# Two-layer encoder trunk on one core: the rings of split weight tiles made four deep and filled by whole tiles, and three unsplit tiles at the head of the second layer's projection

## What is computed

```python
q = einsum(h, w_q); sc = einsum(q, sub_keys)            # 8 heads, 2 sides, 128 keys each
v1, i1 = top_k(sc side 0, 16); v2, i2 = top_k(sc side 1, 16)
top_v, top_pos = top_k(all sums v1 + v2, 16)            # 16 experts of 16384 per head
gates = softmax(top_v)
a = gelu(einsum(u_tab[expert], h)) * gates
out = einsum(a, v_tab[expert])
```

## Time and profile before

| | us |
|---|---|
| median of three runs | 2061.69 |
| lowest, highest | 2059.86, 2061.74 |
| the profiled execution, its own time | 2065.37 |
| its span, first to last instruction | 2063.4 |
| PE, VectorE, ScalarE busy | 2018.4, 1487.8, 1054.8 |
| second expert product, first layer | 360.20 |
| second expert product, second layer | 348.40 |

### The profile page before, as it was taken

How to read it: one execution, slowest core, us unless ns; L and a number is a source line. 1 busy time by engine, 2 the same in 40 slices (tenths; PEclk the granted TensorE clock), 3 DMA queues, 4 the chain that set the end, 5 groups by cost and what they waited for, 6 DMA issues and landing times.

```text
span 2063.4 us, 43464 instructions
## 1 busy us (share of the span) xinstructions
PE 2018.4 (98%) x12678; PEld 1805.7 (88%) x12678; DVE 1487.8 (72%) x3743; ACT 1054.8 (51%) x2059; POOL 27.7 (1%) x56
## 2 busy tenths in 40 slices
PE   7989999999999999999999999999999999999997
PEld 6748899999999877777779689999999998888886
DVE  5662778877777688888875348786777767777776
ACT  2032245755555555555544424566555555555554
POOL 0000000000000000000000000000000000000000
PEclk9999999999999999999989999999999999999998
DMA  9861288865655899999820333777565577777774
GB/s 377 343 236 46 87 279 288 251 189 177 175 171 175 277 325 327 322 328 323 279 102 31 154 117 121 229 219 212 172 176 175 171 207 245 242 240 241 241 242 150
DMA packets 170904, 446.79 MB, mean 217 GB/s; under 512 B 19024, under 2 KB 85840, under 8 KB 166880
## 3 DMA queue, kind: packets, MB, share of 16 engines
q1 hardware_dynamic: 163472, 392.65, 59.6%
q0 software_dynamic: 7376, 53.45, 6.6%
HBM read 409.32 MB, written 36.70 MB: 216 GB/s over the span
## 4 chain that ended last, share of the span: by engine, by line
PE 94%; ACT 2%; DVE 2%; DMA 1%; issue 1%; DVEq 0%; ACTq 0%; SPq 0%
PE bank L492 93%; ACT big L931 1%; DMA big<-in_w_mod 1%; PE bank L631 1%; DVE raw L1097 0%; DVE big L1192 0%; PE bank L811 0%; DMA cst<-in_consts 0%; DVE big L1114 0%; DVE wmod_ring L1114 0%; DVE x_lo L1106 0%; DVE big L1527 0%; ACT L991 0%; ACT big L949 0%; ACT raw L878 0%
## 5 line engine op out<-in xcount | busy, mean ns | idle before, releaser
L1356 DVE TENSOR_TENSOR lo<-raw,hi 128x512 fp32r<-128x512 f32 x1024 | 702.5, 690 | 346.4 <-ACT hi L985 342.1
L985 ACT ACTIVATE hi<-raw 128x512 fp32r<-128x512 f32 x1024 | 642.8, 630 | 444.1 <-PE bank L492 430.2
L492 PE MATMUL bank<-x_hi,hi 128*128 128x256 f32 x2152 | 622.2, 289 | 3.9 <-ACT x_hi L876 1.8
L492 PE MATMUL bank<-x_hi,lo 128*128 128x256 f32 x2152 | 610.1, 283 | 0.0
L492 PE MATMUL bank<-x_lo,hi 128*128 128x256 f32 x2152 | 606.1, 283 | 0.0
L492 PEld LDWEIGHTS bank<-x_hi,hi 128*128 128x128 f32 x2152 | 413.6, 192 | 6.8 <-issue 4.2
L492 PEld LDWEIGHTS bank<-x_hi,lo 128*128 128x128 f32 x2152 | 413.6, 192 | 0.0
L492 PEld LDWEIGHTS bank<-x_lo,hi 128*128 128x128 f32 x2152 | 411.7, 192 | 0.0
L492 PE MATMUL bank<-hi,a_hi 128*128 128x512 f32 x1024 | 401.3, 392 | 3.4 <-issue 1.7
L492 PE MATMUL bank<-hi,a_lo 128*128 128x512 f32 x1024 | 398.8, 389 | 0.0
L492 PE MATMUL bank<-lo,a_hi 128*128 128x512 f32 x1024 | 398.4, 389 | 0.0
(11 more groups left out here) (159 smaller groups left out, 1344.4 us busy)
## 6 DMA issues: line engine op xcount, KB each, us to landing
raw<-in_u SPq DMA_DIRECT2D x256, 512.0 KB, 3.9
raw<-in_v SPq DMA_DIRECT2D x256, 512.0 KB, 4.6
s_store<-work SPq DMA_DIRECT2D x256, 128.0 KB, 3.7
wmod_ring<-s_store SPq DMA_DIRECT2D x256, 128.0 KB, 3.7
wmod_ring<-in_w_mod SPq DMA_DIRECT2D x54, 512.0 KB, 5.7
big<-in_w_mod SPq DMA_DIRECT2D x40, 512.0 KB, 6.3
big<-in_w_q POOLq DMA_DIRECT2D x16, 1024.0 KB, 7.1
big<-in_w_in POOLq DMA_DIRECT2D x6, 2048.0 KB, 14.4
```

The lines of the kernel that those rows point to most:

```text
L492: return nc.tensor.matmul(o, w, x, start=start, stop=stop, skip_group_check=free)
L985: f(hi[:, r % 2, c], raw[:, r, c], ACT.Copy).then_inc(s[l]["hi_done"], 1)
L1356: v.tensor_tensor(lo[:, r % 2, c], raw[:, r, c], hi[:, r % 2, c].bitcast(F32), ALU.subtract).then_inc(s[l]["lo_done"], 1)
```

## The change

`hi` and `lo` become rings of four tiles (`SPLITS`), filled and released by whole tiles; step `n` of ScalarE splits tile `n + 3`. All counts of `hi_done`, `lo_done` and `w_used` are in tiles, and the loops of PE turn over four tiles. In the second expert product the order of VectorE's step stays `weigh`, `lower`, `lower_a`, and `weigh` and `lower_a` stay two steps ahead; `a_hi`, `a_lo` stay rings of two. In the second projection the first three tiles are plain float32 products of the normalised input (which is now written as such), and `x_hi`, `x_lo` are made while they run. The first input weights of the first layer come as 1 MB after four modulation tiles, 1 MB after 15, and the rest from 16 on. The memory for the deeper rings comes from the space that GpSimd's DMA descriptors use (2048 bytes instead of the default).

```diff
-SPLITS = 2
+SPLITS = 4
...
+PLAIN_TILES = 3
...
-                    sp.wait_ge(s[l]["lo_done"], 2 * n - 6)
+                    sp.wait_ge(s[l]["lo_done"], n - 3)
                     load_u(n, n % 4)
...
                 def down_loads(j, i, r, fetches=True):
-                    sp.wait_ge(s[l]["lo_done"], STREAM - 6 + 2 * j)
+                    sp.wait_ge(s[l]["lo_done"], NKEY - 3 + j)
                     load_v(j, r)
                     if fetches:
                         fetch(j + 1, (r + 1) % 4, i + (1 if r == 3 else 0))
...
-                        if n < 3:
-                            pool.wait_ge(s[0]["mod_tile"], (4, EARLY - 2, EARLY)[n])
+                        if n == 0:
+                            pool.wait_ge(s[0]["mod_tile"], 4)
+                            pool.dma_start(big[:, 0:2 * D], w[:, 0:2 * D]).then_inc(win_in[6], 16)
+                            pool.wait_ge(s[0]["mod_tile"], EARLY - 1)
+                            b = 2 * D
+                        if n == 1:
+                            pool.wait_ge(s[0]["mod_tile"], EARLY)
                         pool.dma_start(big[:, b:e], w[:, b:e]).then_inc(win_in[n], 16)
                     pool.dma_start(big[:, BIAS_AT[0]:BIAS_AT[0] + nb], a["bias0"]).then_inc(bias_in, 16)
...
+                for m in range(PLAIN_TILES):
+                    weights_in(m)
+                    for k in range(KT):
+                        if m == 0:
+                            pe.wait_ge(norms["h_ready"], KT * 2 + k + 1)
+                        last = mm(bank[m][:, 0:T], w_qk(1, m, k), hT[:, k, :], k == 0, k == KT - 1)
+                    last.then_inc(s[1]["wt_used"], 1)
+                pe.wait_ge(s[1]["ph_done"], KT)
+                pe.wait_ge(s[1]["pl_done"], KT)
+                for m in range(PLAIN_TILES, QK_TILES[1]):
...
-                    o = bank[4 + r][:, 0:T]
-                    for h in range(2):
-                        pe.wait_ge(s[l]["hi_done"], 2 * n + h + 1)
-                        pe.wait_ge(s[l]["lo_done"], 2 * n + h + 1)
-                        for k in range(h * KT // 2, (h + 1) * KT // 2):
-                            c = slice(k * P, (k + 1) * P)
-                            mm(o, hi[:, r, c], x_hi[:, k, :], k == 0, False)
-                            mm(o, hi[:, r, c], x_lo[:, k, :], False, False)
-                            last = mm(o, lo[:, r, c], x_hi[:, k, :], False, k == KT - 1)
-                        last.then_inc(s[l]["w_used"], 1)
+                    o = bank[4 + r % 2][:, 0:T]
+                    pe.wait_ge(s[l]["hi_done"], n + 1)
+                    pe.wait_ge(s[l]["lo_done"], n + 1)
+                    for k in range(KT):
+                        c = slice(k * P, (k + 1) * P)
+                        mm(o, hi[:, r, c], x_hi[:, k, :], k == 0, False)
+                        mm(o, hi[:, r, c], x_lo[:, k, :], False, False)
+                        last = mm(o, lo[:, r, c], x_hi[:, k, :], False, k == KT - 1)
+                    last.then_inc(s[l]["w_used"], 1)
...
                     pe.wait_ge(s[l]["ah_done"], j + 1)
                     pe.wait_ge(s[l]["al_done"], j + 1)
+                    pe.wait_ge(s[l]["hi_done"], NKEY + j + 1)
+                    pe.wait_ge(s[l]["lo_done"], NKEY + j + 1)
                     for h in range(2):
-                        pe.wait_ge(s[l]["hi_done"], STREAM + 2 * j + h + 1)
-                        pe.wait_ge(s[l]["lo_done"], STREAM + 2 * j + h + 1)
                         c = slice(h * HALF, (h + 1) * HALF)
                         for t in range(TT):
                             o, tok = bank[2 * t + h][:, :], slice(t * P, (t + 1) * P)
-                            mm(o, a_hi[:, r, tok], hi[:, r, c], first, False, True)
-                            mm(o, a_hi[:, r, tok], lo[:, r, c], False, False, True)
-                            last = mm(o, a_lo[:, r, tok], hi[:, r, c], False, end, True)
-                        last.then_inc(s[l]["w_used"], 1)
+                            mm(o, a_hi[:, r % 2, tok], hi[:, r, c], first, False, True)
+                            mm(o, a_hi[:, r % 2, tok], lo[:, r, c], False, False, True)
+                            last = mm(o, a_lo[:, r % 2, tok], hi[:, r, c], False, end, True)
+                    last.then_inc(s[l]["w_used"], 1)
 
                 pe.wait_ge(s[l]["xh_done"], l + 1)
                 pe.wait_ge(s[l]["xl_done"], l + 1)
...
-                if l == 1:
-                    for w in range(2):
-                        for h in range(2):
-                            split_in(w, h)
...
-                def split(n, r, h, round_, wait=True):
+                def split(n, r, round_, wait=True):
                     act.wait_ge(raw_in[r], 16 * (round_ + 1) + 16 * l * (STREAM // RAWS))
                     if wait:
-                        act.wait_ge(s[l]["w_used"], 2 * n + h - 3)
-                    c = slice(h * HALF, (h + 1) * HALF)
-                    f(hi[:, r % 2, c], raw[:, r, c], ACT.Copy).then_inc(s[l]["hi_done"], 1)
+                        act.wait_ge(s[l]["w_used"], n - 3)
+                    f(hi[:, r], raw[:, r], ACT.Copy).then_inc(s[l]["hi_done"], 1)
 
                 def gelu(n, r, round_, wait=True):
-                    act.wait_ge(s[l]["w_used"], 2 * n + 2)
+                    act.wait_ge(s[l]["w_used"], n + 1)
                     if wait:
                         act.wait_ge(s_out[r], 16 * round_ + 16 * l * (NKEY // STAGES))
                     f(work[:, r, :], bank[4 + r % 2][:, 0:T], ACT.Gelu).then_inc(s[l]["s_gelu"], 1)
 
                 def up_step(n, r, round_, wait=True):
-                    nr, nround = (r + 2) % 4, round_ + (r + 2) // 4
-                    split(n + 2, nr, 0, nround)
+                    split(n + 3, (r + 3) % 4, round_ + (r + 3) // 4, wait or r > 0)
                     gelu(n, r, round_, wait)
-                    split(n + 2, nr, 1, nround)
 
                 def up_steps(lo, hi):
...
                 copy_keys(PH - 1)
+                split(2, 2, 0, False)
...
-                def down_step(j, r, round_):
-                    nr, nround = (r + 2) % 4, round_ + (r + 2) // 4 + NKEY // 4
-                    for h in range(2):
-                        split(NKEY + 2 + j, nr, h, nround)
-                    split_a(j + 2, r, nr)
+                def down_step(j, a, r, round_):
+                    if j is not None:
+                        split(NKEY + 3 + j, (r + 3) % 4, round_ + (r + 3) // 4 + NKEY // 4)
+                    split_a(a, r, (r + 2) % 4)
 
                 with act.Fori(0, NKEY // 4 - 1) as i:
                     for r in range(4):
-                        down_step(4 * i + r, r, i)
+                        down_step(4 * i + r, 4 * i + r + 2, r, i)
                 for r in range(2):
...
-                    if i == 2 and k:
-                        lower_x(k - 1)
-                if i == 2:
-                    lower_x(KT - 1)
-
-            def lower_x(k):
-                dve.wait_ge(norms["h_ready"], KT * 2 + k + 1)
-                v.scalar_tensor_tensor(out=x_lo[:, k, :], in0=hT[:, k, :], scalar=mod[1][:, k:k + 1], in1=x_hi[:, k, :].bitcast(F32),
-                                       op0=ALU.add, op1=ALU.subtract).then_inc(s[1]["pl_done"], 1)
...
             def project_split():
+                for k in range(KT):
+                    dve.wait_ge(s[1]["ph_done"], k + 1)
+                    v.tensor_tensor(x_lo[:, k, :], hT[:, k, :], x_hi[:, k, :].bitcast(F32), ALU.subtract).then_inc(s[1]["pl_done"], 1)
                 for w in range(WIN_TILES):
-                    if w + 2 < WIN_TILES:
-                        lower_in(w + 2, 0)
...
-                def lower(n, r, h):
-                    dve.wait_ge(s[l]["hi_done"], 2 * n + h + 1)
-                    c = slice(h * HALF, (h + 1) * HALF)
-                    v.tensor_tensor(lo[:, r % 2, c], raw[:, r, c], hi[:, r % 2, c].bitcast(F32), ALU.subtract).then_inc(s[l]["lo_done"], 1)
+                def lower(n, r):
+                    dve.wait_ge(s[l]["hi_done"], n + 1)
+                    v.tensor_tensor(lo[:, r], raw[:, r], hi[:, r].bitcast(F32), ALU.subtract).then_inc(s[l]["lo_done"], 1)
...
-                    for half in range(2):
-                        lower(NKEY + n, n, half)
+                    lower(NKEY + n, n)
                     lower_a(n, n, n)
-
-                def down_step(j, r, round_, mods=None):
+                lower(NKEY + 2, 2)
+
+                def down_step(j, r, round_, mods=None, left=True):
                     weigh(j + 2, (r + 2) % 4, round_ + (r + 2) // 4)
-                    for half in range(2):
-                        lower(NKEY + 2 + j, (r + 2) % 4, half)
+                    if left:
+                        lower(NKEY + 3 + j, (r + 3) % 4)
                     lower_a(j + 2, r, (r + 2) % 4)
...
-    nc = bacc.Bacc("TRN2", target_bir_lowering=False, num_devices=1)
```

(1 more changed line is left out.)

206 lines of the change are left out of this document (90 added, 116 removed).

## The result

| | before | with the change |
|---|---|---|
| median of four runs, us | 2061.72 | 2092.30 |
| lowest, highest | 2059.86, 2063.20 | 2090.38, 2095.96 |
| profiled execution, its own time and span | 2065.37, 2063.4 | 2095.96, 2094.0 |

The ratio is 1.0151, with a 95% interval of 1.0133 to 1.0169: slower by 30.6 us, where 26 were forecast. The two profiled executions differ by 30.6 us as well, so their traces can be compared stretch by stretch.

The account below looks back on a forecast made before the run. TensorE, busy 98%, bounds the kernel until a three-tile circle through the loads binds in the first layer. +30.2 - 2.6 - 4.5 + 2.7 = +25.8 us on 2065.37 gives 2091.2, as a median 2087.5; range 2070 to 2108.

Parts of the forecast that it names:

- What bounds, and where it changes: Whole kernel: TensorE busy 98% of the span, so time comes only from its pauses, removed work or new waits.
- rival B: Second layer's second expert product: its circle binds too, loads landing after 5.2 us, adding 24 us: 2112; chance 0.14.
- The circle: Second expert product: lower_a, fetch and load issue, landing, split, low part, lower_a three tiles on; 3.53 us plus landing.
- One sign of the prediction: First layer's second expert product: PE pausing at nearly every tile, behind a_hi and a_lo.
- Its price: First layer's second expert product: 390.4 us against 360.2, +30.2, ends +45 and -11.8.
- the guess for the hand-overs: Second expert product's circle: two hand-overs between engines, 0.09 us together, guessed without a row.
- The second layer's margin: Second layer's second expert product: 7.93 us just inside 8.16, so 0, ends 0 and +24.
- The start: Kernel start: 1 MB of w_in held back brings modulation tiles sooner, -2.6 us, ends 0 and -3.5.
- The second projection: Second projection: three plain tiles keep PE busy while x_hi and x_lo are written; 55.9 against 60.4, -4.5 us.
- The start of the first expert product: Both layers: gelu behind late splits delays PE at tile 3; +2.15 and +0.55, together +2.7 us, ends 0 and +5.
- The sum: Whole kernel: +30.2 - 2.6 - 4.5 + 2.7 = +25.8 us, median forecast 2087.5, say 2088.
- A: First layer's second expert product: loads land in time, under 4.48 us, and pauses go; -16.2, so 2045.5 us; chance 0.18.

Follow-up runs that it names:

- the two runs that undo its tie at either end: Changed kernel with load_v issued ahead of fetch on SyncE: 2052.52 us; changed kernel with ScalarE and VectorE taking tile j + 2 instead of j + 3: 2046.21 us.
- The two runs with delays: Changed kernel with one or four 32-byte transfers issued by SyncE ahead of every load_v: 2091.93 us with one, 2183.76 us with four.
- with four delays: Changed kernel with four 32-byte transfers issued by SyncE ahead of every load_v: 2183.76 us, ratio 1.0585.
- the version with four tiles in the circle: Changed kernel with ScalarE and VectorE taking tile j + 2 instead of j + 3 in the second expert product: 2046.21 us, ratio 0.9922.

## Why the prediction was right

The time, 2092.30, lies in the range and 4 us from the forecast of 2088, and the cause was the one named. By its steps:

**What bounds, and where it changes.** Right. Only the stretch that was named changed by much, and rival B's place, the second layer's circle, did not bind: 348.45 against 348.40.

**The circle.** Shown, by the two runs that undo its tie at either end: the load behind `fetch` (one place in SyncE's queue gives 40 us back) and the third tile of lead (taking it away gives 46 us back). The rival of each, the engines' order and the whole tiles, fell with it. The two runs with delays add nothing firm: one small transfer cost nothing, and with four SyncE's queue is the pace. Nor does the sum of 8.16 us in the second layer: it only says that PE sets the pace there. One sign of the prediction was wrong: PE doesn't pause at nearly every tile, but at a third of them.

**Its price.** +30.2 was forecast, +36.2 measured. The step that was mis-sized is the first layer's sum of legs: 9.03 us against 9.36. Of the 0.33, 0.15 lie between split and `lower_a` (2.32 was costed; with four delays, where nothing is in the way, it is 2.24, so the guess for the hand-overs was fair, but in the change other work on the two engines makes it 2.47), 0.14 in the landing, and 0.04 in the issue. A third of 0.33, for 128 tiles, is 14 us; 5 us less for a term that wasn't there (below) and 3 us less because the tiles outside the 110 turns ran faster (396.4 against 3.12 x 128 = 399.4) leave the 6 us. Two of its assumptions were wrong, so that the sum came out as close as it did is in part luck. The landing doesn't follow the mean rate: at 280 and 281 GB/s the medians are 5.5 us and, with one small transfer ahead, 5.1, and a delay that would have cost 27 us by that line cost nothing. And a mean landing isn't what counts: one 512 KB transfer in four tiles makes 39 of the 48 us, and the modulation load, beside it, few. The 0.04 us a tile for VectorE's product, 5 us, wasn't there; cutting the product gave 1 us.

**The second layer's margin.** Right in its result. By its price of 4.3 us for each 0.1 us over the margin of 0.23, a delay of 0.52 us would cost 12 us, and it cost 2.3: most of it was taken up by shorter landings (the leg fell by 0.28 us) and hand-overs (0.16).

**The start.** -2.6 was forecast; PE begins 2.46 us sooner, at 33.94 instead of 36.40. It was then nearly lost in the attention and came back after it: 0.2 us of it are left where the output projection begins and 2.9 where the first expert product does. The granted clock moved: before, 0.97 and then 0.94; with the change, 0.95 and then 1.00.

```profile
100.00:163.55 63.55, 58.08 (x235) 34.09 (x235) 40.61 (x148) 24.43 (x85) 3.13 (x6) 0.97 0.55 207
163.55:217.75 54.20, 53.30 (x268) 46.54 (x267) 12.47 (x29) 11.20 (x24) 0.91 (x2) 0.94 0.16 59
```

```profile
97.60:163.35 65.75, 59.50 (x235) 34.71 (x234) 40.58 (x148) 24.42 (x85) 3.14 (x6) 0.95 0.54 202
163.35:214.85 51.50, 50.18 (x267) 44.37 (x267) 12.47 (x29) 11.08 (x24) 0.77 (x2) 1.00 0.17 62
```

**The second projection.** -4.5 was forecast, 60.9 us before (to the next work at 1129.8) and 56.1 after: -4.8. The 48 plain records run without a pause and at full clock, 10.60 us as costed:

```profile
1102.46 10.60 PE L498 MATMUL bank<-raw,big 128*128 128x256 f32 x48 [0.35 <-ACT raw L876]
```

The norm ahead of it was 1.6 us shorter too, which was not forecast. No half-clock stretch came back here. I didn't undo this part alone, so it rests on the two traces.

**The start of the first expert product.** +2.7 was forecast, +1.8 and +0.4 measured. The place was right: PE waits 1.27 us for a `gelu` at tile 3. The 0.55 us for the second layer came from a misread row: the wait of 1.15 us at 1268.91 belongs to the split whose counterpart in the first layer is at 267.38, with 1.09, and not to tile 4's; that it came out near 0.4 is luck.

**The sum.** 36.2 - 2.9 - 4.8 - 1.6 + 1.8 + 0.4 = 29.1 us; attention and tail of the second layer make up the rest of the 30.6, 1.1 and 0.4.

**The rivals.** A had its price right: the version with four tiles in the circle takes 2046.2 us, where 2045.5 was worked out. Its condition was wrong: landings don't have to be under 4.5 us for that, they were 6.1 in the median; the circle has to be longer. The estimate of 3.2 us for 512 KB from the Trainium skill ("DMA: Bandwidth & Descriptors", "Anatomy of one DMA") is met by no load of `v` in these stretches: the shortest landed in 3.3 us (with the order inside a step turned round, for one), and the lowest median is 3.5, in the second layer with four small transfers. GpSimd's own 512 KB pieces, the kind of transfer that the fit is for, took 5.0 us at the least and 5.5 in the median beside the other loads of the changed kernel.

## What to carry to other kernels

When a ring gets deeper, count over how many tiles each circle closes that goes through **all** queues, the issuing one included: here a weight ring of four became a circle of three, since a short operation for step `m` was put behind the long one for `m + 1` and a load was queued behind that short one. Looking further ahead on the engines of such a circle takes a tile away from it; the cure is to move the load ahead in its queue or to look less far ahead. And where a circle has little slack, the mean latency is a poor measure: ask what one burst in a period does, and expect little from removing one of two. A probe that adds work to a queue must leave the queue room: with four small transfers a tile SyncE itself became the pace, and the run no longer tested what it was made for.
